# Three classic pairs instead of four ahead of the seven-product pairs of a two-layer decoder trunk, with the third pair's low parts made by VectorE and DMA

## The chip, the cores and the metric

The kernel runs on one core of a Trainium2 chip. The time is the device time of one execution in microseconds (us). A profiled execution gives, beside its own time, a trace of every instruction of the engines: TensorE (PE), VectorE (DVE), ScalarE (ACT), GpSimd (POOL) and SyncE (SP, which here only issues transfers).

## The reference

Two layers. Each is a gated feed-forward (SwiGLU, width 2816), a token mixer (a pooling part and a gated linear attention part between two projections), and a second feed-forward, each followed by a residual sum and a layer norm:

```python
D_MODEL = 1024; SEQ = 512; DEPTH = 2; N_META = 16; D_FF = 2816

def swiglu(x, w_gate, w_up, w_down):
    return (jax.nn.silu(x @ w_gate) * (x @ w_up)) @ w_down

for l in range(DEPTH):
    h = layer_norm(a * h + 0.5 * swiglu(h, ffn1_w_gate[l], ffn1_w_up[l], ffn1_w_down[l]), ln1_g[l], ln1_b[l])
    z = h @ w_in[l]
    ...
    y = jnp.concatenate([y_pool, y_gla], axis=-1) @ w_out[l]
    h = layer_norm(a * h + y, ln2_g[l], ln2_b[l])
    h = layer_norm(a * h + 0.5 * swiglu(h, ffn2_w_gate[l], ffn2_w_up[l], ffn2_w_down[l]), ln3_g[l], ln3_b[l])
return h[:, N_META:]
```

All of it is float32, on 528 tokens (16 of them the meta tokens, which the last feed-forward leaves out).

## The kernel before

**Parts.** TensorE multiplies in a rounded float32 form (fp32r). For float32 accuracy each operand is split into a high part (`w_hi`, `x_hi`, `v_hi`, ...: a ScalarE copy that rounds) and a low part (what is left: `w_lo`, `x_lo`, ..., a subtraction), and each product is three: high x high, high x low, low x high.

**Pieces.** The weights come as a stream of pieces of 128 partitions x 1024 columns (512 KB), or 768 where only three blocks of 128 are wanted. SP loads them into the buffers `raw` and `spare`. Piece n uses slot n % 4 of `w_hi` and `w_lo`. Its low part is made in one of these ways, by `kind_of(n)`: "added": ScalarE writes minus the high part's source into `w_lo` and a DMA issued by GpSimd adds the original from memory; "split": GpSimd subtracts, 128x1024 at once (L502); "gate" and "up", the pieces of the fast pairs, below.

**Feed-forward, up to the hidden layer.** The 2816 hidden channels are 22 groups m of 128. For each group there is a gate product and an up product, 128 channels x 528 tokens, over 8 blocks of 128 inputs. A group is a *pair* of pieces. There are two ways:

- *classic* (the first `CLASSIC` groups): both products block by block, 8 blocks x 3 products x 2 token halves x 2 pieces = 96 matrix products. The first three pieces run together, block by block, as the norm ahead delivers its blocks (`chunk_products`). The fourth (`product(3, 3, ...)`) and the later ones run one after the other. In the last feed-forward a product takes all 512 tokens at once, so there are half as many.
- *fast* (`fast_pair`): gate and up, and the two token halves, as a 2 x 2 block product with seven multiplications (Strassen, in Winograd's form) of 4 blocks x 3 products = 84 matrix products. It needs four sums of weight blocks (`s_sum`, made by VectorE in `w_sums`, split by ScalarE in `sum_high` and VectorE in `sum_low`) and four sums of the inputs (`v_sum`, split into `v_hi` and `v_lo`), which are made once in each feed-forward, during the classic pairs. The seven products come in the order p1, p5, p6, p2, p7, p3, p4. Between them TensorE waits for small operations on PSUM: p1's copy (`p1_copied`, ScalarE L1176, wanted ahead of p6), u2's copy (`u2_copied`, L1192, wanted ahead of p7), p5's copy (L1187), and VectorE's sum c22 (L1606, wanted ahead of p4).

The down products of all but the last groups are fast too (three blocks in place of four, 63 products). `FAST_ORDER` lists the fast pairs; a table of two sets of two PSUM bank pairs alternates under them.

**Order.** Every engine runs a list that is written out by hand; semaphores order the engines among each other. ScalarE and VectorE prepare pair i + 1 (copies `gate_high`, `gate_negative`, `up_high`, `sum_high`; `w_sums`, `gate_low`, `sum_low`) while TensorE runs pair i. Each engine is strictly in order, so an operation that waits holds all that stand behind it. SP loads piece n once the piece that had its buffer before is split (`raw_neg`, `lo_done`) and summed (`s_sum_done`).

**Mixer.** TensorE alternates large projections (`project`), small pooling products (`pool_product`), and the attention's parts (`level`, `chunk_updates`, `attend`). Projection idx needs the PSUM bank pair of group idx − 2 empty (`group_free`): 17 needs that of 15, which ScalarE empties (L1359). `chunk_updates(1)` gives the second half of the state, which VectorE scans (`states`, `s_done`); `attend(h)` reads the state of h // 2.

## Time and profile before

| | |
|---|---|
| Time, median of 3 runs | 1845.75 us (1845.32 to 1847.03) |
| The profiled execution's own time | 1843.98 us |
| Its span, first to last instruction | 1842.2 us |
| TensorE busy | 1799.2 us, 14400 products |
| VectorE busy | 1423.8 us |
| ScalarE busy | 1144.9 us |
| GpSimd busy | 357.8 us |
| Mean granted TensorE clock | 0.985 |

Busy times are unions of an engine's instructions; a granted clock of 1 is 2.4 GHz. A row of the timeline gives start, duration (of all, where it stands for several: x2), engine, line, operation, out<-in with the shapes, and in brackets the idle time of the engine ahead of it and what ended that. Line numbers are those of the kernel before.

### The profile page before, as it was taken

The page shows a single profiled execution, that of the slowest core. Times are in us where ns is not written, and L with a number is a line of the kernel's source. Part 1 is how long each engine was busy: PE and PEld are TensorE (multiplying, and loading weights), DVE is VectorE, ACT ScalarE, POOL GpSimd, SP SyncE. Part 2 cuts the span into 40 slices and gives each one's busy share as a digit, 9 for nine tenths or more (in the row PEclk, how much of TensorE's full clock was granted, in tenths as well). Part 3 has the DMA queues.
Part 4 walks back from the last instruction along what each step waited for, and adds up shares of the span by engine and source line. Part 5 has one row for each costly group of instructions (what it writes and reads, how often), then busy time and mean ns, then how long its engine had stood idle before and what let it go on. Part 6 is the DMA issues. An engine that isn't in the chain of part 4 may idle for free.

```text
span 1842.2 us, 37319 instructions
## 1 busy us (share of the span) xinstructions
PE 1799.2 (98%) x14400; PEld 1746.9 (95%) x14400; DVE 1423.8 (77%) x2506; ACT 1144.9 (62%) x1986; POOL 357.8 (19%) x366
## 2 busy tenths in 40 slices
PE   8999999999999999999999999999999999999997
PEld 8999999999999999999999999998997878999996
DVE  6888888668458888888687888886684587888886
ACT  5666666574346667676566666765743465776764
POOL 4121211210012121211321111112100121212113
PEclk9999999899999999999999999999999999999998
DMA  4676757566553576767536767574665636768561
GB/s 162 152 178 133 182 130 166 121 136 134 112 123 91 139 172 138 175 135 167 137 81 144 180 131 179 132 163 126 136 129 115 137 81 152 173 139 186 131 162 70
DMA packets 111264, 259.34 MB, mean 141 GB/s; under 512 B 10480, under 2 KB 37616, under 8 KB 111088
## 3 DMA queue, kind: packets, MB, share of 16 engines
q1 hardware_dynamic: 67600, 167.86, 31.5%
q0 software_dynamic: 43200, 88.10, 28.5%
q8 instruction: 116, 1.90, 0.4%
q10 hardware_dynamic: 288, 0.98, 0.2%
q14 instruction: 60, 0.49, 0.1%
HBM read 254.80 MB, written 2.10 MB: 139 GB/s over the span
## 4 chain that ended last, share of the span: by engine, by line
PE 91%; DVE 4%; ACT 2%; issue 1%; DMA 1%; POOL 0%; ACTq 0%; DVEq 0%
PE PS L621 20%; PE PS L622 20%; PE PS L623 20%; PE PS L600 5%; PE PS L601 4%; PE PS L602 4%; PE PS L557 2%; PE PS L555 2%; PE PS L556 2%; PE PS L565 2%; PE PS L591 2%; PE PS L566 2%; PE PS L912 1%; PE PS L747 1%; DMA raw<-in_stream 1%
## 5 line engine op out<-in xcount | busy, mean ns | idle before, releaser
L495 POOL DMA_DIRECT2D w_lo<-in_stream x300 | 255.8, 853 | 1301.0 <-ACT w_lo L1122 1258.4
L1118 ACT ACTIVATE s_hi<-s_sum 128x512 fp32r<-128x512 f32 (+1 forms) x480 | 280.9, 587 | 158.5 <-PE PS L623 150.4
L1560 DVE TENSOR_TENSOR s_lo<-s_sum,s_hi 128x512 fp32r<-128x512 f32 (+1 forms) x480 | 283.2, 630 | 5.3 <-ACT s_hi L1118 5.3
L621 PE MATMUL PS<-v_hi,s_hi 128*128 128x264 f32 (+1 forms) x864 | 246.0, 285 | 10.8 <-ACT PS L1176 10.8
L623 PE MATMUL PS<-v_hi,s_lo 128*128 128x264 f32 (+1 forms) x864 | 245.2, 284 | 0.0
L622 PE MATMUL PS<-v_lo,s_hi 128*128 128x264 f32 (+1 forms) x864 | 245.0, 284 | 0.0
L600 PE MATMUL PS<-x_hi,w_hi 128*128 128x264 f32 (+1 forms) x696 | 208.1, 299 | 1.7 <-ACT s_r L1359 1.6
L601 PE MATMUL PS<-x_lo,w_hi 128*128 128x264 f32 (+1 forms) x696 | 205.9, 296 | 0.0
L602 PE MATMUL PS<-x_hi,w_lo 128*128 128x264 f32 (+1 forms) x696 | 205.5, 295 | 0.0
L621 PE MATMUL PS<-x_hi,w_hi 128*128 128x264 f32 (+1 forms) x624 | 177.9, 285 | 0.0
L623 PE MATMUL PS<-x_hi,w_lo 128*128 128x264 f32 (+1 forms) x624 | 177.8, 285 | 0.0
L622 PE MATMUL PS<-x_lo,w_hi 128*128 128x264 f32 (+1 forms) x624 | 177.7, 285 | 0.0
L621 PEld LDWEIGHTS PS<-v_hi,s_hi 128*128 128x128 f32 x864 | 163.2, 189 | 11.6 <-ACT PS L1176 11.6
L622 PEld LDWEIGHTS PS<-v_lo,s_hi 128*128 128x128 f32 x864 | 163.7, 189 | 0.0
L1128 ACT ACTIVATE w_hi<-raw 128x1024 fp32r<-128x1024 f32 (+1 forms) x156 | 151.4, 971 | 18.9 <-DMA raw<-in_stream 18.9
L623 PEld LDWEIGHTS PS<-v_hi,s_lo 128*128 128x128 f32 x864 | 163.1, 189 | 0.0
L600 PEld LDWEIGHTS PS<-x_hi,w_hi 128*128 128x128 f32 x696 | 131.1, 188 | 7.4 <-issue 4.2
L1122 ACT ACTIVATE w_lo<-raw 128x512 fp32r<-128x512 f32 (+2 forms) x184 | 135.6, 737 | 0.0
L601 PEld LDWEIGHTS PS<-x_lo,w_hi 128*128 128x128 f32 x696 | 131.2, 188 | 2.7
L602 PEld LDWEIGHTS PS<-x_hi,w_lo 128*128 128x128 f32 x696 | 130.6, 188 | 2.8
L1176 ACT ACTIVATE PS<-PS 128x264 f32<-128x264 f32 (+1 forms) x120 | 44.8, 373 | 130.4 <-PE PS L623 130.4
L1606 DVE TENSOR_TENSOR PS<-PS,p_copy 128x264 f32<-128x264 f32 (+1 forms) x120 | 52.6, 438 | 93.2 <-PE PS L623 93.1
(274 smaller groups left out, 5705.2 us busy)
## 6 DMA issues: line engine op xcount, KB each, us to landing
raw<-in_stream SPq DMA_DIRECT2D x168, 512.0 KB, 4.2
w_lo<-in_stream POOLq DMA_DIRECT2D x144, 256.0 KB, 4.7
spare<-in_stream SPq DMA_DIRECT2D x68, 512.0 KB, 6.9
w_lo<-in_stream POOLq DMA_DIRECT2D x60, 512.0 KB, 7.8
raw<-in_stream SPq DMA_DIRECT2D x48, 384.0 KB, 4.1
spare<-in_stream SPq DMA_DIRECT2D x48, 384.0 KB, 5.3
w_lo<-in_stream POOLq DMA_DIRECT2D x96, 192.0 KB, 4.7
X<-in_x_t SPq DMA_DIRECT2D x8, 264.0 KB, 6.6
```

Of the source, the lines that this page charges most:

```text
L495: pool.dma_start(w_lo[:, slot, to], stream[n // RAWS, n % RAWS, :, part], accum_op=ALU.add).then_inc(lo_added[slot], 16)
L600: yield nc.tensor.matmul(o, hi, rhs_hi[:, k, tok], start=k == 0, stop=False)
L601: yield nc.tensor.matmul(o, hi, rhs_lo[:, k, tok], start=False, stop=False)
L602: yield nc.tensor.matmul(o, lo, rhs_hi[:, k, tok], start=False, stop=k == n - 1)
L621: nc.tensor.matmul(o, hi[:, w], r_hi, start=start and k == 0, stop=False, skip_group_check=True)
L622: nc.tensor.matmul(o, hi[:, w], r_lo, start=False, stop=False, skip_group_check=True)
L623: m = nc.tensor.matmul(o, lo[:, w], r_hi, start=False, stop=stop and k == last, skip_group_check=True)
L1118: nc.scalar.activation(s_hi[:, j - 1, w], s_sum[:, j - 1, w], ACT.Copy).then_inc(S["s_hi_done"], 1)
L1122: nc.scalar.activation(w_lo[:, n % SLOTS, to], of, ACT.Copy, scale=-1.0).then_inc(S["raw_neg"], 1)
L1128: nc.scalar.activation(w_hi[:, n % SLOTS, to], of, ACT.Copy).then_inc(S["raw_hi"], 1)
L1560: V.tensor_tensor(s_lo[:, j - 1, w], s_sum[:, j - 1, w], s_hi[:, j - 1, w].bitcast(F32), ALU.subtract).then_inc(S["s_lo_done"], 1)
L1606: V.tensor_tensor(PS[ps + 1][:, 1, 0:n], PS[ps + 1][:, 0, 0:n], p5_copy[:, 0:n], ALU.add).then_inc(S["c22_done"], 1)
```

## The change

`CLASSIC` becomes 3, so group 3 is a fast pair; each feed-forward has 31 fast pairs in place of 30. The third classic pair's pieces have a new kind, "half": VectorE subtracts the lower four blocks, and ScalarE and a DMA make the upper four by negation and addition; GpSimd does none of the classic ones (it keeps the four pieces of the last down products). TensorE waits for the added half only at block 4. The first fast pair waits for `v_lo` one sum at a time. ScalarE's and VectorE's lists ahead of the first fast pair are written anew, and p1's copy of that pair stands ahead of the copy of the next gate piece. In the mixer `pool_product(16, 3)` moves ahead of `project(17)`, and `attend(0)` no longer waits for the second state update. The bank sets and two spare buffers change places with the parity (`bank_set`, `spare_slot`).

```diff
-CLASSIC = 4
+CLASSIC = 3
...
+def bank_set(i):
+
+    return 2 * ((i + CLASSIC) % 2)
...
-        return "first" if n < SLOTS else "added" if r < SLOTS else "split"
+        return "first" if n < SLOTS else "added" if r < SLOTS else "half" if r < 2 * CLASSIC else "split"
...
 def dma_adds(n):
-    return kind_of(n) in ("added", "gate", "up")
+    return kind_of(n) in ("added", "half", "gate", "up")
 
 
 def engine_splits(n):
-    return kind_of(n) in ("split", "gate")
+    return kind_of(n) in ("split", "half", "gate")
...
                 def mixed(j):
                     if kind == "up":
+                        pe.wait_ge(S["v_lo_done"], 4 * (2 * l + f) + j)
...
-                for m in range(2, CLASSIC):
-                    gate = FP + 2 * m
-                    for j in range(2):
-                        wait_piece(pe, gate + j)
-                        pe.wait_ge(S["prod_done" if j else "silu_done"], F22 + m - 1)
-                        product(2 * (m % 2) + j, (gate + j) % SLOTS, x_hi, x_lo, KC, span=span)\
-                            .then_inc(S["piece_done"], 1)
+                m = CLASSIC - 1
+                for j in range(2):
+                    n = FP + 2 * m + j
+                    wait_low(pe, n)
+                    pe.wait_ge(S["prod_done" if j else "silu_done"], F22 + m - 1)
+                    for k in range(KC):
+                        if k == BAND:
+                            wait_added(pe, n)
+                        for o, tok in matmul_parts(2 * (m % 2) + j, span):
+                            x = tile_products(o, tok, n % SLOTS, k, k, x_hi, x_lo, k == 0, k == KC - 1)
+                    x.then_inc(S["piece_done"], 1)
...
-                    if h < 2:
+                    if h == 0:
                         pe.wait_ge(S["lev_evac"], l * 7 + 7)
+                        pe.wait_ge(S["padded"], l * 3 + 3)
+                    elif h == 1:
                         pe.wait_ge(S["s_done"], l * 2 + 2)
-                        pe.wait_ge(S["padded"], l * 3 + 3)
...
+                pool_product(16, 3)
                 project(17, span)
-                pool_product(16, 3)
...
-                    if follows:
+                    if i > 0 and follows:
                         gate_high(nxt)
                     act.wait_ge(S["p1_acc"], i_all + 1)
...
+                    if i == 0:
+                        gate_high(nxt)
                     if follows:
                         gate_negative(nxt)
                         sum_high(l, f, i + 1, 1)
...
-                    if was == "up" and kind == "up":
+                    if i == 0:
+                        t_low(l, f, 1, span)
+                    elif was == "up" and kind == "up":
                         t_low(l, f, was_a, span)
```

ScalarE in the first feed-forward before, from the third group's silu (the first row) through the first fast pair's copy p1 (L1176) to its u2 copy (L1192):

```order
L1080 ACTIVATE silu<-PS 128x528
L1128 ACTIVATE w_hi<-raw 128x1024
L1122 ACTIVATE w_lo<-raw 128x512
L1092 ACTIVATE h_hi<-prod 128x264
L1128 ACTIVATE w_hi<-raw 128x512
L1122 ACTIVATE w_lo<-raw 128x512
L1118 ACTIVATE s_hi<-s_sum 128x512 x4
L1080 ACTIVATE silu<-PS 128x528
L1092 ACTIVATE h_hi<-h_raw 128x528
L1098 ACTIVATE t_hi<-t_raw 128x1056
L1128 ACTIVATE w_hi<-raw 128x1024
L1176 ACTIVATE PS<-PS 128x264
```

The same place in the changed kernel, whose L1094 is the silu, L1106 h_hi, L1112 t_hi, L1142 a high copy of weights, L1136 a negated copy, L1132 s_hi, L1197 p1's copy, L1210 and L1215 those of p5 and u2:

```order
L1094 ACTIVATE silu<-PS 128x528
L1112 ACTIVATE t_hi<-t_raw 128x1056
L1132 ACTIVATE s_hi<-s_sum 128x512 x2
L1106 ACTIVATE h_hi<-prod 128x264
L1197 ACTIVATE PS<-PS 128x264
L1142 ACTIVATE w_hi<-raw 128x1024
L1136 ACTIVATE w_lo<-raw 128x512
L1132 ACTIVATE s_hi<-s_sum 128x512
L1210 ACTIVATE p_copy<-PS 128x264
L1215 ACTIVATE u_copy<-PS 128x264
```

The fourth group's silu, h_hi and t_hi are gone from ahead of p1's copy, and the gate copy (128x1024) stands behind it; an s_hi of the second fast pair still stands ahead of the copies of p5 and u2.

VectorE in the changed kernel, from the second product's last t_raw to the first s_sum of the second fast pair (L1561 to L1570 are s_sum, L1577 a gate's w_lo, L1548 v_lo, L1583 s_lo, L1450 a product of silu and up, L1481 h_lo):

```order
L1570 TENSOR_TENSOR s_sum<-s_sum,raw 128x512
L1577 TENSOR_TENSOR w_lo<-raw,w_hi 128x512
L1548 TENSOR_TENSOR v_lo<-v_sum,v_hi 128x1056
L1583 TENSOR_TENSOR s_lo<-s_sum,s_hi 128x512 x2
L1450 SCALAR_TENSOR_TENSOR prod<-PS,silu 128x528
L1548 TENSOR_TENSOR v_lo<-v_sum,v_hi 128x1056
L1583 TENSOR_TENSOR s_lo<-s_sum,s_hi 128x512 x2
L1481 TENSOR_TENSOR h_lo<-h_raw,h_hi 128x528
L1481 TENSOR_TENSOR h_lo<-prod,h_hi 128x264
L1561 TENSOR_TENSOR s_sum<-spare 128x512
```

Before, at the same distance from the first fast pair, VectorE had:

```order
L1547 TENSOR_TENSOR s_sum<-s_sum,raw 128x512
L1554 TENSOR_TENSOR w_lo<-raw,w_hi 128x512
L1560 TENSOR_TENSOR s_lo<-s_sum,s_hi 128x512 x4
L1427 SCALAR_TENSOR_TENSOR h_raw<-PS,silu 128x528
L1441 TENSOR_TENSOR t_raw<-h_raw,prod 128x264
L1442 TENSOR_TENSOR t_raw<-prod 128x264
L1444 SCALAR_TENSOR_TENSOR t_raw<-t_raw,prod 128x264
L1447 SCALAR_TENSOR_TENSOR t_raw<-t_raw,h_raw 128x264
L1458 TENSOR_TENSOR h_lo<-h_raw,h_hi 128x528
L1468 TENSOR_TENSOR t_lo<-t_raw,t_hi 128x1056
L1538 TENSOR_TENSOR s_sum<-spare 128x512
```

Two of the four v_lo now lie between the first fast pair's sums, and the second group's h_lo behind them; its t_lo moves into the first fast pair, and the fourth group's work into the second.

## Rows read from the trace of the kernel before

**Rows 1.** The page, busy time, share of the span and instructions of each engine

```profile
PE 1799.2 (98%) x14400; PEld 1746.9 (95%) x14400; DVE 1423.8 (77%) x2506; ACT 1144.9 (62%) x1986; POOL 357.8 (19%) x366
```

**Rows 2.** Waits of TensorE: for whom, us in total, times, longest

```profile
PE PS L621 <- ACT PS L1176: 10.8, 4, 3.7
...
PE PS L946 <- issue: 1.8, 2, 0.9
PE PS L600 <- ACT s_r L1359: 1.6, 2, 0.8
```

**Rows 3.** Timeline of TensorE, second feed-forward: two pieces, two fast pairs

```profile
608.33 0.28 PE L600 MATMUL PS<-x_hi,w_hi 128*128 128x264 f32 x1
...
614.12 0.28 PE L621 MATMUL PS<-x_hi,w_hi 128*128 128x264 f32 x1
...
619.60 0.39 PE L621 MATMUL PS<-v_hi,s_hi 128*128 128x264 f32 x1 [2.38 <-ACT PS L1176]
...
628.50 0.28 PE L621 MATMUL PS<-x_hi,w_hi 128*128 128x264 f32 x1
...
638.67 0.28 PE L621 MATMUL PS<-x_hi,w_hi 128*128 128x264 f32 x1
```

**Rows 4.** Stretches: us, busy times of the engines, granted clock, DMA share

```profile
614.00:629.00 15.00, 12.62 (x92) 12.41 (x91) 11.59 (x21) 8.57 (x14) 1.70 (x2) 0.89 0.77 212
```

**Rows 5.** Timeline of TensorE, first and last feed-forward, the same places

```profile
53.85 0.28 PE L621 MATMUL PS<-x_hi,w_hi 128*128 128x264 f32 x1
...
66.65 0.28 PE L621 MATMUL PS<-x_hi,w_hi 128*128 128x264 f32 x1
...
1522.55 0.40 PE L600 MATMUL PS<-x_hi,w_hi 128*128 128x512 f32 x1
...
1528.11 0.28 PE L621 MATMUL PS<-x_hi,w_hi 128*128 128x256 f32 x1
...
1543.53 0.28 PE L621 MATMUL PS<-x_hi,w_hi 128*128 128x256 f32 x1
...
1553.47 0.28 PE L621 MATMUL PS<-x_hi,w_hi 128*128 128x256 f32 x1
```

**Rows 6.** Timeline of ScalarE, second feed-forward

```profile
584.84 0.61 ACT L1080 ACTIVATE silu<-PS 128x528 f32<-128x528 f32 x1 [1.63 <-PE PS L591]
...
586.29 2.06 ACT L1110 ACTIVATE v_hi<-v_sum 128x1056 fp32r<-128x1056 f32 x2
...
618.23 1.04 ACT L1128 ACTIVATE w_hi<-raw 128x1024 fp32r<-128x1024 f32 x1
619.17 0.37 ACT L1176 ACTIVATE PS<-PS 128x264 f32<-128x264 f32 x1
```

**Rows 7.** Timeline of VectorE and GpSimd, second feed-forward

```profile
590.38 3.34 DVE L1519 SCALAR_TENSOR_TENSOR v_sum<-v_sum,X 128x1056 f32<-128x1056 f32 x1
...
600.42 2.42 DVE L1525 TENSOR_TENSOR v_lo<-v_sum,v_hi 128x1056 fp32r<-128x1056 f32 x2
...
589.68 2.92 POOL L502 TENSOR_TENSOR w_lo<-raw,w_hi 128x1024 fp32r<-128x1024 f32 x1 [0.81 <-ACT w_hi L1128]
```

**Rows 8.** The same, operations back to back, and a DMA issue beside them

```profile
598.18 0.69 DVE L1427 SCALAR_TENSOR_TENSOR h_raw<-PS,silu 128x528 f32<-128x528 f32 x1
...
609.26 0.69 DVE L1538 TENSOR_TENSOR s_sum<-raw 128x512 f32<-128x512 f32 x1 [0.89 <-DMA raw<-in_stream]
...
614.88 0.70 DVE L1427 SCALAR_TENSOR_TENSOR h_raw<-PS,silu 128x528 f32<-128x528 f32 x1
...
610.70 0.86 POOL L495 DMA_DIRECT2D w_lo<-in_stream  x1 [4.79 <-ACT w_lo L1122]
```

**Rows 9.** The page, DMA issues: KB each, median us from issue to landing

```profile
raw<-in_stream SPq DMA_DIRECT2D x168, 512.0 KB, 4.2
w_lo<-in_stream POOLq DMA_DIRECT2D x144, 256.0 KB, 4.7
```

**Rows 10.** Timeline of VectorE, first mixer: the last pooling input

```profile
465.94 0.68 DVE L1890 SCALAR_TENSOR_TENSOR ft<-win,ft 128x512 f32<-128x512 f32 x1
```

115 lines of the change are left out of this document (63 added, 52 removed).

## The prediction

> **What bounds the kernel now.** The page first: TensorE is busy for 98% of the span [rows 1], so only fewer matrix products or fewer of its waits can move the time. Then the waits of TensorE alone [rows 2]: one group recurs once in each of the four feed-forwards, 10.8 us in all (L621 behind ScalarE's L1176), and two recur once in each of the two mixers, 1.6 and 1.8 us.
>
> A matrix product's record is 0.28 us long, but the next starts 0.12 us after it, so an idle time in a row is about 0.16 us shorter than what the wait displaces. I therefore measure from start to start. In the second feed-forward a classic piece (half a pair) takes 614.12 − 608.33 = 5.79 us; the first fast pair takes 628.50 − 614.12 = 14.38, the second 638.67 − 628.50 = 10.17 [rows 3]. The first loses 4.21 us, though only 2.38 stand as idle in its row: the rest is clock. In 614 to 629 the granted clock is 0.89, that is, TensorE fell from 2.4 to 1.2 GHz for some 1.6 us after the idle time [rows 4]. In the first feed-forward the first fast pair takes 66.65 − 53.85 = 12.80, a loss of 2.63. In the last, whose rows are 512 and 256 wide, a classic piece takes 5.56, the first fast pair 15.42, the second 9.94: a loss of 5.48 [rows 5]. The third repeats the second's rows to within 0.01 us. **Sum of the losses: 2.63 + 4.21 + 4.22 + 5.48 = 16.5 us.**
>
> Why does TensorE wait there? It needs the copy p1 (L1176), and ScalarE starts that at 619.17, directly behind the whole copy of the second pair's gate piece, 618.23, 0.94 us long [rows 6], itself behind the hidden pieces of the fourth pair. Those were late because VectorE was.
>
> **Why VectorE was late.** It shares something with GpSimd. A 128x1056 operation takes 1.2 us (two in 2.42), but the one at 590.38 takes 3.34, while GpSimd's subtraction runs 589.68 to 592.60 [rows 7]. So VectorE lost 2.1 us there, and the trace has two more such losses in each feed-forward. The Trainium skill ("SBUF — State Buffer", Terms) says that the two hold a port pair exclusively, for a whole instruction, the loser waiting fully: by that rule the row would be 592.60 − 590.38 + 1.25 = 3.5, and it is 3.34.
>
> **The change, part by part.**
>
> 1. *One classic pair fewer.* 96 products become 84 (7 sums of 4 blocks, 3 products each). From the rows: 2 x 5.79 − 10.17 = 1.41 us in three feed-forwards and 2 x 5.56 − 9.94 = 1.18 in the last [rows 3, 5]. Together **−5.4 us**. No operation of it is hidden: it is on TensorE.
>
> 2. *The old wait at the first fast pair*, **−16.5 us** as summed, provided ScalarE and VectorE keep up with a classic phase one pair shorter. What is late next is item 3.
>
> 3. *The new wait.* I lay the second feed-forward's order on a clock whose zero is the start of the fourth classic piece (before, five pieces of 5.8 us ahead of 614.12, so 585.1). ScalarE starts its first silu at −0.3 [rows 6]. Then it has silu 0.5, gate copy 0.94, its negation 0.5, two v_hi copies 1.95, h_hi 0.3: h_hi(0) ends at +4.05. VectorE idles until then, and has from there no wait that I can find: h_lo 0.4; two v_sum 2.5; a w_lo 0.6; two v_lo 2.4; the second product with its four t_raw 2.24 (600.42 − 598.18); nine operations 128x512 took 614.88 − 609.26 = 5.62, so 0.62 each: four s_sum 2.6 (one of them waits for the one before it) and one w_lo 0.6; a v_lo 1.3; two s_lo 1.2; the third product 0.65; a v_lo 1.25; two s_lo 1.2; h_lo(1), h_lo(2) 0.95; then the first s_sum of the second fast pair 0.7 [rows 7, 8]. Sum 18.6, so that sum is ready at +22.65. Behind it ScalarE has in its queue s_hi 0.55, p5's copy 0.35 and u2's copy 0.4, ready at +23.95. TensorE is through three classic pieces (17.4) and four products of 1.455 at +23.2, and needs the u2 copy. **Stall 0.75 us.** In the last feed-forward TensorE is there at 3 x 5.56 + 4 x 1.42 = 22.4 and the chain is some 0.3 shorter: 1.3 us. Together 3 x 0.75 + 1.3 = **+3.5 us**. In the second fast pair VectorE then has a heavy share (product, four t_raw, t_lo), and arrives with c22 within 0.2 us of TensorE's need: the same backlog, not a second one. Bounds: nothing (the chain 4% shorter), and 2 us per feed-forward more (a tenth longer, where the clock could fall again).
>
> 4. *The copy p1 ahead of the gate copy.* It takes 0.94 us off the copy's path; inside item 2. Here p1's copy is asked for at 17.4 + 1.6 = 19.0, and ScalarE waits for the third product, at +18.5, before it: free, with 0.5 us to spare.
>
> 5. *GpSimd, DMA and the queues.* Of eight subtractions per feed-forward four go; two are taken by VectorE (0.6 us each for half a piece, counted above) and by two accumulating DMAs of 256 KB. The third pair's gate add is issued at +1.8 and wanted at 5.8 + 2.9 = 8.7, since only the upper four blocks wait for it; such adds land in 4.7 us at the median: slack 2.2 [rows 9]. SP can load the first fast pair's up piece only after VectorE's second w_lo, at +7.7; with 4.2 us to land it is there at +11.9, wanted at +12.1 [rows 9]. That is the tightest of the loads: each us more is a us on VectorE's chain. Nothing added.
>
> 6. *The mixer.* `pool_product(16, 3)` now stands between projects 15 and 17, which share a PSUM bank set. Its input was finished at 465.94 + 0.68 [rows 10], 3.5 us before TensorE gets there, and it lasts 1.0 us, over the time in which ScalarE empties the bank. And `attend(0)` no longer waits for the second state update, which only its successors' bank needs. The two waits go: 1.6 + 1.8 idle, plus 4 x 0.16: **−4.0 us** [rows 2].
>
> **Sum:** −5.4 − 16.5 − 4.0 + 3.5 = −22.4 us. The profiled execution took 1843.98, which makes 1821.6; the median of the runs shown is 1.77 above it, so **1845.75 − 22.4 = 1823.3 us**.
>
> **Rivals.**
>
> *A, the likeliest (0.62)*: new stalls of 0.3 to 1.8 us per feed-forward, 1820.5 to 1827.5.
>
> *B, VectorE keeps up (0.13)*: every saving, no new stall: 1845.75 − 25.9 = 1819.8. For it: the chain needs only 0.75 us less, and my durations are rounded up. Against: in the last feed-forward 1.3 would have to go.
>
> *C, GpSimd's DMA issues hold VectorE as its subtractions did (0.13).* An issue's record is 0.86 us, and four lie along the chain: 3.4 us more, a stall of 4.2 per feed-forward. That gives 1823.3 + 13.7 = 1837.0, and with a fallen clock in three of the four (1.6 each) 1841.8. Against it: the issue at 610.70 lies in the midst of the nine operations that took 0.62 us each [rows 8]. The Trainium skill ("SBUF — State Buffer", Terms) has GpSimd write the descriptors of such DMAs, and it is by the exclusive port pair that one would expect this; the trace has VectorE at its usual pace. Something milder of this sort gives 1828 to 1836.
>
> *D, the mixer's edits do nothing (0.08)*, because something else ends just as late there (the level sums' evacuation, another bank): +4.0, 1827.3. For it: the profile calls the releaser of L946 only "issue". Against: in the code nothing else that is late stands between.
>
> *E, slower (0.02)*: the loads of the first fast pair's up piece come too late. Slack is 0.2 us, and every us beyond it delays the sums, the s_hi and s_lo behind them, and so TensorE. It decides when each feed-forward loses more than 25.9 / 4 = 6.5 us, a landing of 11 us after the issue, where the median is 4.2; to be slower by 0.2% (3.7 us) it takes 12. At 13 us, stalls of 8.6 + 0.75 give some 1857 with the halved clock.
>
> **How the numbers follow.** The remaining 0.02 lies within 0.2%, about what a measurement of this kernel tells from no change (3.7 us). The range runs from B to the milder part of C: 1819 to 1830; it leaves out the rest of C and E. Faster 0.96, same 0.02, slower 0.02.
>
> **What would show each step.** (1) First fast pair minus a second one: 0.3 to 1.8 us, not 2.6 to 5.5, its wait now behind the u2 copy and not behind p1's. (2) Granted clock 1.0 there. (3) VectorE's 128x1056 operations at 1.25 us beside the GpSimd queue, none at 3.3. (4) No wait at the successor of L946 or at project 17. (5) Two classic pieces fewer, 11.6 us, and one pair of 10.2 more. The prediction is wrong if VectorE finds a wait in its chain that I don't see (for a raw piece, above all), if a stall halves the clock again, or if the second fast pair's c22 is late by more than the first's backlog.

## The result, and the profile after

The changed kernel takes **1823.62 us** at the median (1822.08 to 1826.83, 4 runs), beside 1845.59 us (1845.32 to 1847.03, 4 runs) for the kernel before, run beside it: a ratio of 0.9882, with a 95% interval of 0.9865 to 0.9899, or 22 us less. In two later series the changed kernel was run again: 1824.14 beside 1844.92 (0.9887, interval 0.9872 to 0.9901) and 1823.22 beside 1844.68 (0.9877, 0.9860 to 0.9893). The forecast was 1823.3.

The profiled execution is the slowest of the changed kernel's four: its own time is 1826.83, its span 1825.1. First its page, busy time, share of the span and instructions of each engine, beside [rows 1]:

```profile
PE 1796.3 (98%) x14400; PEld 1745.5 (96%) x14400; DVE 1426.1 (78%) x2558; ACT 1163.6 (64%) x2030; POOL 327.4 (18%) x366
...
raw<-in_stream SPq DMA_DIRECT2D x164, 512.0 KB, 4.3
w_lo<-in_stream POOLq DMA_DIRECT2D x160, 256.0 KB, 4.6
```

TensorE's number of products is the same by an accident of counting. In each of the first three feed-forwards there are 12 fewer (2864 between two layer norms, 2876 before); in the last a classic product is 512 wide and a fast one 256, so that the pair that became fast has 36 more, and 36 − 3 x 12 = 0. GpSimd is busy 30 us less, VectorE 2 us more although it has 52 operations more, because operations that were stretched to 3.3 us are short again. Sixteen accumulating adds of 256 KB are new, as the last line has it (144 before, [rows 9]).

The waits of TensorE (for whom; us in total, times, the longest), beside [rows 2]:

```profile
PE PS L575 <- DVE w_lo L2065: 5.3, 1, 5.3
PE PS L631 <- ACT u_copy L1215: 4.0, 4, 1.4
...
PE PS L631 <- ACT PS L1197: 0.2, 1, 0.2
```

The wait behind p1's copy (L1176 before, L1197 now) has gone from 10.8 us to 0.2. Both of the mixers' waits, 1.8 and 1.6 us, are gone. The one new wait recurs once in each feed-forward and stands behind u2's copy, where the forecast had put it. The 5.3 us of the first line are the start of the kernel and are no news.

The timeline of TensorE: the first product of the first fast pair and of the second, in the first, second, third and last feed-forward (columns: start, duration, engine, line, operation), beside [rows 3, 5]:

```profile
42.45 0.28 PE L631 MATMUL PS<-x_hi,w_hi 128*128 128x264 f32 x1
...
53.50 0.28 PE L631 MATMUL PS<-x_hi,w_hi 128*128 128x264 f32 x1
...
598.53 0.28 PE L631 MATMUL PS<-x_hi,w_hi 128*128 128x264 f32 x1
...
606.13 0.39 PE L631 MATMUL PS<-v_hi,s_hi 128*128 128x264 f32 x1 [1.36 <-ACT u_copy L1215]
...
609.17 0.31 PE L631 MATMUL PS<-v_hi,w_hi 128*128 128x264 f32 x1
...
610.66 0.28 PE L631 MATMUL PS<-x_hi,w_hi 128*128 128x264 f32 x1
...
620.84 0.28 PE L631 MATMUL PS<-x_hi,w_hi 128*128 128x264 f32 x1
...
953.45 0.28 PE L631 MATMUL PS<-x_hi,w_hi 128*128 128x264 f32 x1
...
964.74 0.28 PE L631 MATMUL PS<-x_hi,w_hi 128*128 128x264 f32 x1
...
1505.25 0.28 PE L631 MATMUL PS<-x_hi,w_hi 128*128 128x256 f32 x1
...
1517.59 0.28 PE L631 MATMUL PS<-x_hi,w_hi 128*128 128x256 f32 x1
```

The first fast pairs take 11.05, 12.13, 11.29 and 12.34 us; a second one takes 620.84 − 610.66 = 10.18, and 9.96 in the last feed-forward. What they lose is 0.88 + 1.96 + 1.12 + 2.38 = **6.3 us**, against 16.5 before and 3.5 in the forecast. Counted from start to start, 5.0 of it lie at the product that needs u2's copy, and 0.75 at the one that needs p1's, in the second and the last feed-forward. (The waits' 4.0 us are idle time alone: each displaces 0.27 us more than its row says, where the forecast took 0.16.) The granted clock in those stretches (columns: stretch, its length, busy times, the granted clock, DMA share, GB/s), beside [rows 4]:

```profile
598.53:610.66 12.13, 10.77 (x86) 10.38 (x85) 11.59 (x19) 7.86 (x15) 1.70 (x2) 1.00 0.80 232
...
1505.25:1517.59 12.34, 10.75 (x85) 10.21 (x84) 11.91 (x19) 8.22 (x16) 1.70 (x2) 1.00 0.80 232
```

It stayed at 2.4 GHz, where in the second feed-forward before it had fallen. So the whole 6.3 us is waiting. What is late? VectorE's timeline along the chain that the forecast had laid out:

```profile
585.21 0.44 DVE L1481 TENSOR_TENSOR h_lo<-prod,h_hi 128x264 fp32r<-128x264 f32 x1 [2.08 <-ACT h_hi L1106]
585.56 1.25 DVE L1539 SCALAR_TENSOR_TENSOR v_sum<-v_sum,X 128x1056 f32<-128x1056 f32 x1
586.85 1.26 DVE L1542 SCALAR_TENSOR_TENSOR v_sum<-v_sum,X 128x1056 f32<-128x1056 f32 x1
588.03 0.69 DVE L1577 TENSOR_TENSOR w_lo<-raw,w_hi 128x512 fp32r<-128x512 f32 x1
...
594.39 0.69 DVE L1561 TENSOR_TENSOR s_sum<-raw 128x512 f32<-128x512 f32 x1 [1.10 <-DMA raw<-in_stream]
...
604.17 0.69 DVE L1561 TENSOR_TENSOR s_sum<-spare 128x512 f32<-128x512 f32 x1
...
608.58 0.44 DVE L1636 TENSOR_TENSOR PS<-PS,p_copy 128x264 f32<-128x264 f32 x1
```

And ScalarE's, where that chain hands over to TensorE:

```profile
604.89 0.63 ACT L1132 ACTIVATE s_hi<-s_sum 128x512 fp32r<-128x512 f32 x1 [1.85 <-DVE s_sum L1561]
605.43 0.37 ACT L1210 ACTIVATE p_copy<-PS 128x264 f32<-128x264 f32 x1
605.70 0.38 ACT L1215 ACTIVATE u_copy<-PS 128x264 f32<-128x264 f32 x1
```

h_lo(0), the low part of group 0's hidden values, at 585.21, the first s_sum of the second fast pair at 604.17, s_hi behind it at 604.89, the two copies, and TensorE at 606.13: link by link the forecast's chain. It is 18.96 us from h_lo(0) to the start of the s_sum; the forecast had 17.9 (18.6 less the sum's own 0.7). The difference is one entry, which the forecast had weighed and set to nothing: VectorE waited 1.10 us for the raw up piece, whose load was issued at 588.79. The view of that tile over the stretch of this one load gives its landing:

```profile
L480 SPq DMA_DIRECT2D raw<-in_stream x1: 328/328/328, 588.8 to 588.8; - x1
...
DMA to landing us min/median/max: 5.5/5.5/5.5
```

5.5 us, where the page's median is 4.3.

### The profile page after: what moved, and what is told of

Read it like the earlier page. It is cut to its first block, busy times and chain, and to the rows that moved or that the text cites. A ratio compares the mean times of both kernels' runs of the same rounds, so it can differ in the third digit from the quotient of the medians.

```text
span 1825.1 us, 37497 instructions
## 1 busy us (share of the span) xinstructions
PE 1796.3 (98%) x14400; PEld 1745.5 (96%) x14400; DVE 1426.1 (78%) x2558; ACT 1163.6 (64%) x2030; POOL 327.4 (18%) x366
## 4 chain that ended last, share of the span: by engine, by line
PE 91%; DVE 5%; ACT 2%; issue 1%; DMA 1%; ACTq 0%; DVEq 0%; SPq 0%
PE PS L631 20%; PE PS L632 20%; PE PS L633 20%; PE PS L610 3%; PE PS L611 3%; PE PS L612 3%; PE PS L567 3%; PE PS L565 3%; PE PS L566 3%; PE PS L575 2%; PE PS L601 2%; PE PS L576 2%; PE PS L925 1%; PE PS L760 1%; DMA raw<-in_stream 1%
## 5 line engine op out<-in xcount | busy, mean ns | idle before, releaser
L505 POOL DMA_DIRECT2D w_lo<-in_stream x316 | 269.3, 852 | 1412.4 <-ACT w_lo L1136 1377.4
L1132 ACT ACTIVATE s_hi<-s_sum 128x512 fp32r<-128x512 f32 (+1 forms) x496 | 291.2, 588 | 160.2 <-PE PS L633 145.0
L1583 DVE TENSOR_TENSOR s_lo<-s_sum,s_hi 128x512 fp32r<-128x512 f32 (+1 forms) x496 | 294.0, 634 | 2.9 <-ACT s_hi L1132 2.6
L631 PE MATMUL PS<-v_hi,s_hi 128*128 128x264 f32 (+1 forms) x912 | 259.3, 284 | 4.2 <-ACT u_copy L1215 4.0
L632 PE MATMUL PS<-v_lo,s_hi 128*128 128x264 f32 (+1 forms) x912 | 257.8, 283 | 0.0
L633 PE MATMUL PS<-x_hi,w_lo 128*128 128x264 f32 (+1 forms) x656 | 185.6, 283 | 0.0
L631 PE MATMUL PS<-x_hi,w_hi 128*128 128x264 f32 (+1 forms) x656 | 185.5, 283 | 0.0
L632 PE MATMUL PS<-x_lo,w_hi 128*128 128x264 f32 (+1 forms) x656 | 185.5, 283 | 0.0
L1142 ACT ACTIVATE w_hi<-raw 128x1024 fp32r<-128x1024 f32 (+2 forms) x152 | 147.2, 968 | 7.9 <-DMA raw<-in_stream 7.9
L1136 ACT ACTIVATE w_lo<-raw 128x512 fp32r<-128x512 f32 (+2 forms) x196 | 142.9, 729 | 0.0
L610 PE MATMUL PS<-x_hi,w_hi 128*128 128x264 f32 (+1 forms) x472 | 141.1, 299 | 0.1
L611 PE MATMUL PS<-x_lo,w_hi 128*128 128x264 f32 (+1 forms) x472 | 138.9, 294 | 0.0
L612 PE MATMUL PS<-x_hi,w_lo 128*128 128x264 f32 (+1 forms) x472 | 138.7, 294 | 0.0
L1197 ACT ACTIVATE PS<-PS 128x264 f32<-128x264 f32 (+1 forms) x124 | 46.3, 373 | 136.3 <-PE PS L633 136.3
L633 PE MATMUL PS<-x_hi,s_lo 128*128 128x264 f32 (+1 forms) x448 | 127.8, 285 | 0.0
L632 PE MATMUL PS<-x_lo,s_hi 128*128 128x264 f32 (+1 forms) x448 | 127.1, 284 | 0.0
L631 PE MATMUL PS<-x_hi,s_hi 128*128 128x264 f32 (+1 forms) x448 | 127.0, 283 | 0.0
```

The source lines that it names most:

```text
L505: pool.dma_start(w_lo[:, slot, to], stream[n // RAWS, n % RAWS, :, part], accum_op=ALU.add).then_inc(lo_added[slot], 16)
L610: yield nc.tensor.matmul(o, hi, rhs_hi[:, k, tok], start=k == 0, stop=False)
L611: yield nc.tensor.matmul(o, hi, rhs_lo[:, k, tok], start=False, stop=False)
L612: yield nc.tensor.matmul(o, lo, rhs_hi[:, k, tok], start=False, stop=k == n - 1)
L631: nc.tensor.matmul(o, hi[:, w], r_hi, start=start and k == 0, stop=False, skip_group_check=True)
L632: nc.tensor.matmul(o, hi[:, w], r_lo, start=False, stop=False, skip_group_check=True)
```

## The experiments

Eight variants were run, and the changed kernel twice more, in three series, each series beside the kernel before. The first four variants take the change apart.

**1. Is it the mixer's two edits that took the two waits away, and what are they worth?** (For rival D.) Both are undone in the changed kernel:

```diff
-                    if h == 0:
+                    if h < 2:
                         pe.wait_ge(S["lev_evac"], l * 7 + 7)
-                        pe.wait_ge(S["padded"], l * 3 + 3)
-                    elif h == 1:
                         pe.wait_ge(S["s_done"], l * 2 + 2)
+                        pe.wait_ge(S["padded"], l * 3 + 3)
...
-                pool_product(16, 3)
                 project(17, span)
+                pool_product(16, 3)
```

> The changed kernel with the mixer's two edits undone. By my theory their two waits return (project 17 behind ScalarE's s_r, L946 behind the second state update), 1.03 and 1.05 us from start to start in each of two mixers: 4.1 us more than the changed kernel, 1827.7 against a median of 1823.6, and the feed-forwards as they are. By the rival (the mixer edits only moved a wait to another place) the time stays at 1823.6.

Measured: 1828.32 us (1826.85 to 1829.41), ratio 0.9905 (0.9890 to 0.9920) to the kernel before of its series. Its waits of TensorE:

```profile
PE PS L631 <- ACT u_copy L1215: 4.1, 4, 1.4
...
PE PS L959 <- issue: 1.8, 2, 0.9
PE PS L610 <- ACT s_r L1381: 1.6, 2, 0.8
```

Both waits are back to the tenth of a us, and the wait behind u2's copy has not moved (4.1 us, beside 4.0). By the ratios the edits are worth (0.9905 − 0.9882) x 1845.6 = 4.2 us, but the two intervals overlap (0.9890 to 0.9920 and 0.9865 to 0.9899), so the times alone don't show it. The traces do: from the layer norm ahead of a mixer to the one behind it, this variant takes 203.19 and 199.24 us, where three executions of the changed kernel take 200.91 and 197.48 at the mean. That is 2.3 + 1.8 = 4.0 us. Rival D falls.

**2. What does the order of ScalarE's copies do alone?** In the kernel before, with its four classic pairs, p1's copy is put ahead of the gate copy in the first fast pair:

```diff
-                    if follows:
+                    if i > 0 and follows:
                         gate_high(nxt)
...
+                    if i == 0:
+                        gate_high(nxt)
```

> The kernel before with one edit alone: p1's copy of each first fast pair ahead of the copy of the next gate piece. By my theory the old wait was mostly VectorE's lateness (ScalarE reached the gate copy late, behind the fourth pair's h_hi and t_hi), so the copy gains only the 0.94 us of the gate copy per feed-forward, plus what of the clock's fall goes with it: the idle time at L621 falls from 2.4 to 1.45 us, 1839.5 to 1842. By the rival (the copy's place was the cause) the first fast pair loses its whole 16.5 us, 1829.

Measured: 1838.04 us (1836.33 to 1839.38), ratio 0.9958 (0.9943 to 0.9973), some 8 us less, where moving a copy past 0.94 us of work four times is 3.8. Its wait behind p1 is 7.1 us, 10.8 − 7.1 = 3.7 less. The clock gives more on top: 0.93 us less idle time in the second feed-forward made its first fast pair 14.38 − 12.01 = 2.4 us shorter, and the third did the same. But in the last one the pair is 0.2 us longer than before (15.65 beside 15.42), although its idle time is 0.92 us shorter. The four first fast pairs are 0.9 + 2.4 + 2.3 − 0.2 = 5.3 us shorter in all, 3.7 of it idle time and 1.6 clock. The profiled executions differ by 5.6 us; the other 2.5 of the medians' 8 stand in no trace, and the interval allows 5 to 10.5. Two stretches of this kernel around the first fast pair, in the second and the last feed-forward, and under them one of the kernel before, in the last:

```profile
610.00:625.00 15.00, 13.55 (x111) 13.33 (x111) 13.95 (x25) 10.44 (x18) 1.76 (x3) 1.00 0.80 211
...
1520.00:1535.00 15.00, 12.24 (x70) 11.57 (x69) 12.68 (x22) 8.86 (x16) 2.56 (x3) 0.77 0.73 202
```

```profile
1530.50:1545.50 15.00, 11.32 (x83) 11.12 (x82) 11.72 (x21) 8.86 (x16) 1.70 (x2) 0.89 0.70 194
```

The idle time in the second feed-forward is 1.45 us now and the clock stays at 2.4 GHz (before 2.38 and 0.89, [rows 3, 4]); in the last it is 2.76 and the clock falls to 1.2 GHz for a longer part (0.77) than it did before after 3.68 us (0.89). The measured median lies 1.5 us under the expected range, which had kept a part of the fallen clock.

**3. What is it worth that the third pair's low parts are VectorE's and the DMA's?** In the changed kernel GpSimd computes them whole; VectorE's two w_lo, ScalarE's negations and the two adds go:

```diff
-        return "first" if n < SLOTS else "added" if r < SLOTS else "half" if r < 2 * CLASSIC else "split"
+        return "first" if n < SLOTS else "added" if r < SLOTS else "split"
...
-                gate_high(FP + 4)
-                gate_negative(FP + 4)
+                whole_high(FP + 4)
...
-                gate_low(FP + 4)
                 h_low(l, f, 0, span)
                 v_sums(l, f, span, (2, 4))
-                gate_low(FP + 5)
```

> The changed kernel with the third pair's low parts by GpSimd again, whole pieces, and without VectorE's two w_lo and ScalarE's two negations. By my theory VectorE loses some 2.1 us beside the second subtraction (one v_sum of 3.3 in place of 1.25 us) and wins 0.6 for its own w_lo: the first sum of the second fast pair comes 0.4 to 1.5 us later in each feed-forward, 1825 to 1830. By the rival (the new kernel is late because of loads and adds, not VectorE) the two adds of 256 KB that go let the up piece land in 4.1 us in place of 5.5 and the time falls to 1820.

Measured: 1826.17 us (1825.02 to 1827.45), ratio 0.9894 (0.9879 to 0.9909), some 2 us above the changed kernel, within the intervals of both. Its VectorE, and under it its GpSimd, at the same place:

```profile
584.35 0.49 DVE L1477 TENSOR_TENSOR h_lo<-prod,h_hi 128x264 fp32r<-128x264 f32 x1 [2.50 <-ACT h_hi L1104]
584.75 1.25 DVE L1535 SCALAR_TENSOR_TENSOR v_sum<-v_sum,X 128x1056 f32<-128x1056 f32 x1
586.04 3.34 DVE L1538 SCALAR_TENSOR_TENSOR v_sum<-v_sum,X 128x1056 f32<-128x1056 f32 x1
589.30 2.42 DVE L1544 TENSOR_TENSOR v_lo<-v_sum,v_hi 128x1056 fp32r<-128x1056 f32 x2
...
593.87 0.68 DVE L1557 TENSOR_TENSOR s_sum<-raw 128x512 f32<-128x512 f32 x1
```

```profile
585.35 2.91 POOL L512 TENSOR_TENSOR w_lo<-raw,w_hi 128x1024 fp32r<-128x1024 f32 x1 [0.81 <-ACT w_hi L1140]
```

With the subtraction back, the v_sum beside it is back at 3.34 us, to the hundredth what it was [rows 7]; without it the same operation takes 1.26. So GpSimd's subtraction is shown as the cause of this stretched operation, one of the three in each feed-forward before, by taking it out and putting it in. It is not shown as the whole of VectorE's lateness. The Trainium skill ("SBUF — State Buffer", Terms) has the two engines hold their shared port pair for a whole instruction and the loser wait: by it the row would be 585.35 + 2.91 − 586.04 + 1.25 = 3.47. The trace agrees to 0.13. But the profit is small: the first fast pairs lose 1.70, 1.76, 1.77 and 2.32 us here, 7.6 in all, against 6.3 (and 5.5, the mean of three executions of the changed kernel). For VectorE's first s_sum of the up piece starts 9.5 us behind h_lo(0) (593.87 − 584.35) with the slow operation and 9.2 us (594.39 − 585.21) without it. The 2.1 us freed went into the w_lo that VectorE took over (0.6) and into the wait for the load (1.10), which this variant does not have. And h_lo(0) itself starts 13.8 us ahead of the first fast pair here (598.18 − 584.35) and 13.3 us ahead of it in the changed kernel (598.53 − 585.21), where ScalarE makes a negated copy before the h_hi that VectorE waits for.

**4. Is that load's wait the difference to the forecast?** In the changed kernel VectorE computes the w_lo that frees the load's buffer one operation earlier:

```diff
-                v_sums(l, f, span, (2, 4))
+                v_sums(l, f, span, (2,))
                 gate_low(FP + 5)
+                v_sums(l, f, span, (4,))
```

> The changed kernel with VectorE's w_lo of the third pair's up piece one v_sum (1.2 us) earlier, so that SP can load the first fast pair's up piece 1.2 us earlier. The trace of the changed kernel has VectorE waiting 1.1 us for that piece in the second feed-forward. By my theory that wait goes and the wait for the u2 copy shrinks by as much, some 1 us where it stands: 1820 to 1822.5. By the rival (the load ends late because the adds occupy the queues) it lands at the same time and nothing changes, 1823.6.

Measured: 1822.22 us (1819.33 to 1822.43), ratio 0.9873 (0.9856 to 0.9889). VectorE at the same place, and TensorE's wait:

```profile
582.44 0.43 DVE L1481 TENSOR_TENSOR h_lo<-prod,h_hi 128x264 fp32r<-128x264 f32 x1 [2.09 <-ACT h_hi L1106]
...
583.96 0.68 DVE L1577 TENSOR_TENSOR w_lo<-raw,w_hi 128x512 fp32r<-128x512 f32 x1
...
590.39 0.69 DVE L1561 TENSOR_TENSOR s_sum<-raw 128x512 f32<-128x512 f32 x1
```

```profile
PE PS L631 <- ACT u_copy L1215: 1.9, 4, 0.8
```

No wait for the load is left in any feed-forward, though this one, too, took 5.6 us to land. The first fast pairs lose 0.63, 0.71, 0.75 and 1.15 us, 3.2 in all: about the forecast's 0.75 three times and 1.3. So the forecast had the length of VectorE's chain right, and was wrong in the load. The ratios (0.9873 here, 0.9882 for the changed kernel) don't tell the two kernels apart; it is the waits that do.

**5 to 8. Is the order at the end of the chain what makes it a wait?** The changed kernel again, and three variants. In the second of them ScalarE's p5 and u2 copies stand ahead of the late s_hi; in the third VectorE's c22 stands ahead of two s_lo as well; the fourth adds the early load. The diff of the fourth, in its parts, without the lines of experiment 4:

```diff
                         gate_negative(nxt)
-                        sum_high(l, f, i + 1, 1)
+                        if i > 0:
+                            sum_high(l, f, i + 1, 1)
...
                     if follows:
+                        if i == 0:
+                            sum_high(l, f, i + 1, 1)
                         sum_high(l, f, i + 1, 2)
...
-                        sum_low(l, f, i + 1, 1)
-                        sum_low(l, f, i + 1, 2)
+                        if i > 0:
+                            sum_low(l, f, i + 1, 1)
+                            sum_low(l, f, i + 1, 2)
...
+                    if i == 0:
+                        sum_low(l, f, i + 1, 1)
+                        sum_low(l, f, i + 1, 2)
```

> The changed kernel once more, without an edit, to stand beside the three variants of this series. Its median was 1823.6 us, but its profiled execution took 1826.8 and its span 1825.1. My account of those 3 us is that TensorE stayed at the lower clock for longer behind the layer norms in that one execution (the time lost around each norm was 4.6 to 6.0 us against 3.5 to 4.7 in the kernel before), and not that the kernel has a slow place. So another profiled execution should have a span of 1820 to 1823 and the same lengths of the first fast pairs: 11.0, 12.1, 11.3, 12.3 us to 0.3 us each. The rival, that the losses at the first fast pairs themselves differ from one execution to another (the load of the up piece landing now after 4.2 us and now after 5.5), would show different lengths, 10.9 where the load comes early.

> In the first fast pair ScalarE copies p5 and u2 before it computes s_hi(1,1), which waits for VectorE's s_sum; nothing else is changed. In the changed kernel TensorE's only wait in a feed-forward is behind that u2 copy (4.0 us in all, 1.4 the longest), and the copy itself needs nothing of the late sum: it stands behind s_hi in ScalarE's queue. Theory 1, mine: the copy was the wait that ended last, but only just; VectorE's own chain is late by nearly as much, and its first block operation (c22, at 608.58 in the second feed-forward, which starts as soon as VectorE is free) is needed by the product that comes next. The wait moves there: the first fast pair loses 0.2 to 0.6 us less than now, 1821.5 to 1823 us, and the page shows a wait behind c22 or s_lo in place of the one behind the copy. Theory 2: the copy alone was late; then nothing waits in the first fast pair, the 6.3 us that the four lose go but for 0.3 each, and the time is 1818 us. Theory 3: s_hi(1,1), now later by 0.7 us, is itself what TensorE needs next; then the time is the same as now or 0.5 us over it.

> As the run before, and VectorE too computes the first fast pair's c22 ahead of s_lo(1,1) and s_lo(1,2). This takes both of TensorE's next needs out from behind the late sum. Theory 1: the first fast pair loses 0.3 to 0.6 us in place of 0.9 to 2.4, so 4 us come back; but VectorE's backlog is not smaller for it, and it ends only in the third fast pair, so what is pushed back (s_lo(1,2), and with it the second fast pair's c22, which has 0.2 us to spare now) takes 0 to 2 us of it: 1819 to 1822 us, with a wait behind s_lo or behind the second fast pair's c22 on the page. Theory 2: the order is all there is to it, the backlog fits: 1818 us.

> The order of the run before together with the early load (VectorE's gate_low(FP+5) between the two v_sum of the first fast pair), which by itself gave 1822.2 us and first fast pairs that lose 0.63 to 1.15 us each, 3.2 in all. If the load and the order are two cures of one lateness, they add only to the point where nothing is late: first fast pairs of 10.3 to 10.6 us, losses of 0.2 to 0.4 each, and 1818 to 1820.5 us, the fastest of all. If the order of the run before costs at the second fast pair, the early load takes a microsecond off VectorE's backlog there too, and this run is faster than that one by up to 2 us. If the early load's own gain of 3 us was noise of one series, it equals the run before.

Measured, beside 1844.92 us (7 runs) for the kernel before; the losses are those of the first and second fast pairs, in the four feed-forwards, in us:

| kernel | median (range) | ratio (interval) | first fast pairs lose | second |
|---|---|---|---|---|
| changed, again | 1824.14 (1823.46–1826.07) | 0.9887 (0.9872–0.9901) | 0.91, 1.21, 0.78, 1.93 = 4.8 | 0 |
| copies first | 1824.17 (1822.13–1826.25) | 0.9885 (0.9871–0.9900) | 0.80, 2.30, 1.09, 2.67 = 6.9 | 0 |
| copies and c22 first | 1822.32 (1821.62–1822.97) | 0.9875 (0.9860–0.9890) | 0.04, 0.27, 0.04, 0.42 = 0.8 | 0.36, 0.73, 0.45, 0.87 = 2.4 |
| the early load too | 1820.99 (1818.76–1823.14) | 0.9868 (0.9851–0.9884) | 0.03, 0.04, 0.04, 0 = 0.1 | 0.14, 0.34, 0.36, 0.84 = 1.7 |

The changed kernel again: a span of 1822.6, as expected. Its lengths are not the same to 0.3 us, though: the second, third and last feed-forward differ by 0.75, 0.35 and 0.5 us. So the rival of that expectation holds as well, the load lands now sooner and now later. Its VectorE row, beside 1.10 above:

```profile
592.84 0.69 DVE L1561 TENSOR_TENSOR s_sum<-raw 128x512 f32<-128x512 f32 x1 [0.36 <-DMA raw<-in_stream]
```

0.74 us less waiting for the load (it landed in 4.8 us), 0.75 us less in the first fast pair (12.13 and 11.38).

With the copies first nothing is gained. TensorE's wait has moved by two products, to the one that needs c22. TensorE, and VectorE in the same kernel:

```profile
608.75 0.36 PE L631 MATMUL PS<-v_hi,w_hi 128*128 128x264 f32 x1 [1.44 <-issue]
```

```profile
608.22 0.43 DVE L1639 TENSOR_TENSOR PS<-PS,p_copy 128x264 f32<-128x264 f32 x1
```

The profile names no releaser, but VectorE's c22 ends at 608.65, 0.1 us before. The same could be read in the changed kernel above: c22 from 608.58 to 609.02, the product that needs it at 609.17, without a wait in its row only because the wait for u2's copy had come just before. The expected 0.2 to 0.6 us (1821.5 to 1823) did not show: my theory was right in where the wait goes, and wrong in that something comes back at all. Nor is anything lost. The 6.9 us are more than 4.8 because the load came later in this execution: VectorE waits 0, 1.43, 0.23 and 1.28 us for it. Less that, the losses are 0.80, 0.87, 0.86 and 1.39, those of the changed kernel.

With c22 first as well the first fast pairs are all but free, and a part of the lateness, 2.4 us, turns up one pair later, again without a releaser:

```profile
616.86 0.36 PE L631 MATMUL PS<-v_hi,w_hi 128*128 128x264 f32 x1 [0.48 <-issue]
```

VectorE's c22 of that pair runs from 616.32 to 616.75. That is the forecast's "arrives with c22 within 0.2 us of TensorE's need" in the second fast pair, made late by what was pushed back. But only a part turns up there. With VectorE's waits for the load taken off, the first two fast pairs of the four feed-forwards lose 3.9 us in the changed kernel, 3.9 with the copies first, 3.2 with the early load, 2.3 with c22 first too, and 1.8 with all three. So an order that puts everything that TensorE needs next ahead does give some 1.5 us back. The time of all three together, 1820.99 us, is 3.2 us below the changed kernel's of its series, the lowest of all medians; the two intervals overlap (0.9851 to 0.9884 and 0.9872 to 0.9901), so that it is the fastest is likely and not shown. The expectations of the last two, 1819 to 1822 and 1818 to 1820.5, were missed by 0.3 and 0.5 us.

**9 and 10. Does a later load cost what an early one gives?** VectorE's w_lo ahead of the load is put one operation later, and the changed kernel is run a third time beside it.

```diff
                 v_sums(l, f, span, (2, 4))
-                gate_low(FP + 5)
                 v_low(l, f, span, 1)
+                gate_low(FP + 5)
                 v_low(l, f, span, 2)
```

> The opposite of the early load: VectorE's gate_low(FP+5), on which the load of the first fast pair's up piece waits, stands behind v_low(1) and not ahead of it, so that the load is issued 1.2 us later and nothing else is moved by more than one operation. So far two executions of the changed kernel showed that load landing in 5.5 and in 4.8 us in the second feed-forward, VectorE waiting 1.10 and 0.36 us for it, and the first fast pair taking 12.13 and 11.38 us: 0.75 us of the load made 0.75 us of TensorE. Theory 1, mine (the wait of the first fast pair is the landing of this load, passed on one for one): VectorE waits 1.2 us more, 1.5 to 2.4 us in each feed-forward, and each first fast pair takes 1.2 us more than in the changed kernel, 12.2 to 13.5; that is 4.9 us in all, 1829 us, and where TensorE's idle time comes to 2.4 us or more the clock falls and 1.6 us is added, in up to three of the four: up to 1834 us. Theory 2 (it is the length of VectorE's own chain, and the wait for the load is only where its slack shows): the time stays within 1.5 us of the changed kernel's.

> The changed kernel a third time, beside the run with the late load: 1822.5 to 1825 us, a span of 1820 to 1825, VectorE's wait for the up piece's load in the second feed-forward between 0.3 and 1.2 us, and the first fast pair there 11.0 us and that wait together, within 0.1 us.

Measured: 1824.00 us (1822.98 to 1828.08) with the late load, ratio 0.9890 (0.9875 to 0.9905), and 1823.22 (1820.55 to 1823.45) without. Time and span of the latter are as expected; its VectorE did not wait for the load in the second feed-forward, where 0.3 to 1.2 us were expected, and the first fast pair took 11.16 us. By its numbers my theory falls: 1829 to 1834 was expected, and the time moved by less than 1 us. VectorE of the kernel with the late load, and the landing:

```profile
592.50 0.69 DVE L1561 TENSOR_TENSOR s_sum<-raw 128x512 f32<-128x512 f32 x1 [0.92 <-DMA raw<-in_stream]
```

```profile
DMA to landing us min/median/max: 4.2/4.2/4.2
```

The load was issued 1.2 us later behind h_lo(0), and landed in 4.2 us, where the same load in the changed kernel's three executions took 5.5, 4.8 and 4.6 (and 5.6 when issued early). So a later issue was hardly a later landing. What did hold is the link behind it. In the sixteen feed-forwards of these four executions VectorE's wait for the load and the first fast pair's loss go together:

| execution | wait for the load | first fast pair loses | difference |
|---|---|---|---|
| changed, first | 0, 1.10, 0.23, 1.01 | 0.88, 1.96, 1.12, 2.38 | 0.88, 0.86, 0.89, 1.37 |
| changed, again | 0, 0.36, 0, 0.53 | 0.91, 1.21, 0.78, 1.93 | 0.91, 0.85, 0.78, 1.40 |
| changed, third | 0, 0, 0, 1.65 | 0.74, 0.99, 0.93, 2.66 | 0.74, 0.99, 0.93, 1.01 |
| late load | 0.21, 0.92, 0.20, 0.60 | 0.99, 1.76, 1.03, 1.96 | 0.78, 0.84, 0.83, 1.36 |

The last column is what the forecast called the new stall: 0.75 in the first three feed-forwards, 1.3 in the last. A wait for the load of nothing to 1.65 us comes on top of it, one for one within some 0.2 us; only in the last feed-forward of the third execution does less of it arrive (1.01 in place of 1.4). Why does the later issue cost nothing? GpSimd issues an accumulating add shortly ahead of this load, in the changed kernel's first execution at 586.94, and the variants change the distance between the two. From the issues and landings of all four feed-forwards:

| kernel | load issued behind the add | the load lands in | the add lands in |
|---|---|---|---|
| early load | 0.5 us | 4.8, 5.6, 5.6, 4.7 | 5.9 to 6.1 |
| changed, three executions | 1.8 us | 4.3 to 5.9, mean 4.8 | 4.0 to 4.5 |
| late load | 3.0 us | 3.5, 4.2, 3.4, 3.8 | 4.1 to 4.3 |

Issued 1.2 us later, the load lands 1.1 us sooner after its issue, and where the two are issued together both are slow. So its landing is no fixed time: how much of the add is still under way goes with a good part of it. That the two share DMA engines would explain this; it was not tried by itself. The spread at one and the same distance, 4.3 to 5.9 us in the changed kernel, stays unexplained.

## Why the prediction was right, point by point

1. *One classic pair fewer, −5.4.* Not tried alone. What the ratios leave for it and for VectorE's lateness is 22 − 8 (the copy, experiment 2) − 4 (the mixer, 1) − 2 (the low parts, 3) = 8 us. The edits depend on each other, so this is an account and no measurement. One stretch bears on the term itself: the first feed-forward is 3.0 us shorter (table below), its first fast pair loses 1.8 us less, and 1.2 us are left, beside the forecast's 1.41.
2. *The old wait, −16.5.* Gone: 0.2 us of idle time are left of it, and the granted clock is 1.00 there, as the forecast had it. One reading in the sum's source was off: a granted clock of 0.89 over 15 us is a loss of some 1.6 us, and at half speed that is some 3.3 us at 1.2 GHz, not 1.6. The loss, and so the term, stay the same.
3. *The new wait, +3.5.* **The term that was mis-sized: 5.5 us, the mean of the three executions (6.3, 4.8, 5.3).** Place, releaser and the chain's length were right: without VectorE's waits for the load the losses come to 3.9 us. The other 1.6 are those waits. The step that failed is "with 4.2 us to land it is there at +11.9, wanted at +12.1", with nothing added. It stood on the page's median. This load is one that starts among other transfers, and in the twelve feed-forwards of the three executions it took 4.3 to 5.9 us; the forecast itself had called it the tightest. Luck had a small part in the chain: its five ScalarE terms add up to +3.9 from −0.3, not to the +4.05 written; the trace has h_lo(0) at +4.05.
4. *The copy p1 ahead.* Right but for the "free": the product behind p1's copy starts 0.5 us late in the last feed-forward and 0.2 us in the second. Alone the edit measured 8 us (5 to 10.5), a third of the whole; the traces show 5.3, of which 1.6 is clock.
5. *GpSimd, DMA, queues, nothing.* No stretched operation is left in the chain (1.25 and 1.26 us for the two v_sum), so C falls: an add's issue by GpSimd from 586.94 to 587.80 lies inside the v_sum of 586.85, which took 1.26, and in none of the three executions does any VectorE operation of this chain take longer. The load is in point 3.
6. *The mixer, −4.0.* Measured 4.0 by the traces, 4.2 by the ratios.

**The sum, by stretches.** The first product of each layer norm cuts the span in seven. Start of that product, before and in the three executions of the changed kernel, and the stretch between two of them:

| stretch up to | before | changed, three executions | mean difference | forecast |
|---|---|---|---|---|
| first norm (feed-forward 1) | 355.94 | 352.94, 353.23, 352.77 | −3.0 | −3.3 |
| second (a mixer) | 203.28 | 201.31, 201.15, 200.26 | −2.4 | −2.0 |
| third (feed-forward 2) | 358.59 | 355.86, 354.17, 353.92 | −3.9 | −4.9 |
| fourth (feed-forward 3) | 358.60 | 354.07, 353.70, 353.86 | −4.7 | −4.9 |
| fifth (a mixer) | 199.83 | 198.14, 197.11, 197.19 | −2.4 | −2.0 |
| last (feed-forward 4) | 349.42 | 347.35, 346.83, 347.98 | −2.0 | −5.4 |
| end | 16.54 | 15.43, 16.41, 15.62 | −0.7 | 0 |

The forecast's column is its own terms, −1.41 − 2.63 + 0.75 and so on; the differences add up to −19.1, the mean of the spans less 1842.2. Six stretches are within 1 us. The last feed-forward gave 3.4 us less than forecast: 1 us is the load (point 3), and 1.5 the clock behind the norm at its start; 0.9 is not accounted for. The stretch of 20 us from some 6 us before that norm, in the kernel before and in the changed kernel's first and second execution:

```profile
1470.00:1490.00 20.00, 16.45 (x88) 13.08 (x88) 16.58 (x34) 13.01 (x20) 1.70 (x2) 1.00 0.62 133
```

```profile
1456.00:1476.00 20.00, 17.94 (x79) 14.33 (x78) 15.26 (x32) 11.91 (x19) 1.70 (x2) 0.74 0.56 124
```

```profile
1453.00:1473.00 20.00, 17.94 (x79) 14.20 (x78) 15.55 (x33) 12.21 (x19) 1.71 (x2) 0.74 0.59 130
```

TensorE did 88 products in the one and 79 in the others. The change does not touch the norm, and over the twelve profiles of this study (before, changed and variants) this clock is 0.74 in four, 0.83 in four, 0.91 in two and 1.00 in two, one of which has nearly all of the change (experiment 3). It was 0.74 in all three executions of the changed kernel, so whether its order has a part in it stays open; that an unchanged place varies by this much is shown. The profiled execution of the kernel before had the lucky case: it took 1843.98 where its medians are 1844.7 to 1846.2. A forecast that compares one profile with another carries such 2 us. The medians, which don't, moved by 22.0, 20.8 and 21.5 us, mean 21.4, where the forecast says 22.4; the missing 1.0 is about half of point 3's 2.0. The very small miss of the median, 0.3 us, was thus partly luck.

*The rivals.* B: no, a new stall is there in all of 12 feed-forwards. C: no (point 5). D: no (experiment 1). E: its mechanism, the up piece's load, is real, at 0 to 1.65 us and not at the 6.5 from which it decides. (Its landing times are 0.75 us too high by the forecast's own sum, since the stall of 0.75 is there already: 6.5 us are reached by a landing of some 10 us. The 1857 at 13 us holds no fallen clock.)

## What to carry to other kernels

Where a forecast lays out a chain and finds a load with 0.2 us to spare, the page's median landing is not its price: take a landing of that tile in the same neighbourhood of transfers, and carry its spread in the sum, since here each us that VectorE waited for it went nearly one for one into TensorE's wait. And a load beside other transfers is no fixed time behind its issue: 1.2 us later in the list cost next to nothing. When the engine that computes is late by a backlog, a new order among what waits for it can only move the wait to the next product (experiment 6, nothing gained). It gives something back when all that is needed next stands ahead, and then a part turns up one pair later (experiment 7). And shorten first those stalls after which the clock falls: in experiment 2, 0.9 us less waiting was worth 2.3 to 2.4 in two of the four places, though nothing in the last, where the clock fell even so.

## What the runs showed of the hardware

What a stall costs in clock could be seen from both sides, and the idle time alone does not decide it. After idle times of 1.36 to 1.53 us in the first fast pair (the changed kernel and experiment 2) TensorE kept 2.4 GHz. After 2.38 (granted clock 0.89 over 15 us, [rows 4]) and 2.76 us (0.77, experiment 2) it had fallen to 1.2 GHz for a time. Nor did the length of the slow time follow the idle time: after 3.68 us, in the last feed-forward of the kernel before, the granted clock was 0.89 over 15 us, and after 2.76 us, at the same place in experiment 2, 0.77. And after 2.34 us, in the first feed-forward of the kernel before, the clock had not fallen:

```profile
54.00:69.00 15.00, 12.66 (x105) 12.45 (x104) 13.02 (x24) 9.28 (x16) 1.70 (x2) 1.00 0.78 208
```

Behind the layer norms, where TensorE idles and has short products, the granted clock over the same 20 us differed from one execution to the next of one and the same kernel (0.83 and 0.74 at the second norm of the changed kernel), about 1 us each time.

The other is the landing time: one and the same load of 512 KB, at the same distance from its neighbours, landed in 5.5, 4.8 and 4.6 us in three executions. Issued 0.5 us behind an accumulating add of 256 KB it took 4.7 to 5.6 us and the add about 6; issued 3.0 us behind, it took 3.4 to 4.2 and the add about 4.2.

The third is what VectorE and GpSimd do to each other. In experiment 3 the subtraction that starts at 585.35, inside a v_sum of VectorE, takes 2.91 us, where GpSimd's subtractions take 2.40 at the median of that execution; and the v_sum behind it takes 3.34 in place of 1.25. DMA issues of 0.84 to 0.86 us by GpSimd stretch none of VectorE's operations beside them in the changed kernel's chain.
